# Turning the attention maps of seven units by 32 by 32 squares and two DRAM buffers, in the neighbourhood attention layer

## The reference, cut to what matters

```
q, k, v, g = jnp.split(h @ w_in, 4, axis=-1)           # 16 heads of 64, 4 rows of 64 positions
s_loc = einsum(q, keys in the window) + rpb bias        # 4 rows x 16 columns around the query
s_ctx = einsum(q, kc)                                   # 256 context keys
p = softmax(concat([s_loc, s_ctx]))
o = p_loc @ v + p_ctx @ vc
y = (o * silu(g)) @ w_out
```

## Time and profile before

| | us |
|---|---|
| median of 3 runs | 1815.25 (1814.78 to 1815.6) |
| the profiled execution | 1815.61 |
| its span | 1813.8 |
| DVE busy | 954.2 |
| ACT busy | 901.5 |
| POOL busy | 1366.0 |

### The profile page before, as it was taken

How to read it: one execution, slowest core, us unless ns; L and a number is a source line. 1 busy time by engine, 2 the same in 40 slices (tenths; PEclk the granted TensorE clock), 3 DMA queues, 4 the chain that set the end, 5 groups by cost and what they waited for, 6 DMA issues and landing times.

```text
span 1813.8 us, 24988 instructions
## 1 busy us (share of the span) xinstructions
PE 1793.3 (99%) x9274; PEld 1477.5 (81%) x9274; DVE 954.2 (53%) x1756; ACT 901.5 (50%) x1329; POOL 1366.0 (75%) x568
## 2 busy tenths in 40 slices
PE   6999999999999999999999999999999999999999
PEld 5888888887889888887788888888888878888887
DVE  4673766778755524866653230713095876143152
ACT  3324424674455644456554644464445565555452
POOL 2624544559968898977689798969897867888885
PEclk9999999999999999999999999999999999999999
DMA  9863885749775775565665566567655666656663
GB/s 366 291 210 94 270 310 163 198 141 312 244 277 200 211 221 191 180 198 168 209 186 192 179 195 191 193 187 234 191 193 185 192 190 182 196 160 210 190 195 128
DMA packets 206457, 372.91 MB, mean 206 GB/s; under 512 B 33508, under 2 KB 59092, under 8 KB 205780
## 3 DMA queue, kind: packets, MB, share of 16 engines
q1 hardware_dynamic: 203328, 363.69, 63.5%
q10 hardware_dynamic: 3028, 7.86, 1.2%
HBM read 367.27 MB, written 9.28 MB: 208 GB/s over the span
## 4 chain that ended last, share of the span: by engine, by line
PE 97%; DVE 2%; DMA 0%; issue 0%; ACTq 0%; ACT 0%; POOL 0%; DVEq 0%
PE ps L1300 26%; PE ps L1302 25%; PE ps L1301 25%; PE ps L1426 3%; PE ps L1427 3%; PE ps L1428 3%; PE ps L1992 1%; PE ps L1993 1%; PE ps L1994 1%; PE ps L1348 1%; PE ps L1697 1%; PE ps L1918 1%; PE ps L1668 1%; PE ps L1678 1%; PE ps L1962 1%; PE ps L1558 1%
## 5 line engine op out<-in xcount | busy, mean ns | idle before, releaser
L659 POOL TENSOR_TENSOR w_lo<-raw,w_hi 128x1024 fp32r<-128x1024 f32 x556 | 1347.1, 2461 | 397.4 <-ACT w_hi L697 376.2
L1300 PE MATMUL ps<-w_hi,act_rows_r 128*128 128x512 f32 x2064 | 814.8, 395 | 3.2 <-POOL w_lo L659 3.1
L1302 PE MATMUL ps<-w_hi,act_rows_r 128*128 128x512 f32 x2064 | 805.2, 390 | 0.0
L1301 PE MATMUL ps<-w_lo,act_rows_r 128*128 128x512 f32 x2064 | 804.6, 390 | 0.0
L697 ACT ACTIVATE w_hi<-raw 128x1024 fp32r<-128x1024 f32 x556 | 571.1, 1058 | 371.0 <-DMA raw<-in_ffn_w_up 100.8
L1300 PEld LDWEIGHTS ps<-w_hi,act_rows_r 128*128 128x128 f32 x2064 | 388.2, 188 | 90.4 <-issue 9.1
L1302 PEld LDWEIGHTS ps<-w_hi,act_rows_r 128*128 128x128 f32 x2064 | 388.0, 188 | 82.0
L1301 PEld LDWEIGHTS ps<-w_lo,act_rows_r 128*128 128x128 f32 x2064 | 388.4, 188 | 77.7
L2647 DVE STREAM_TRANSPOSE ps<-proj 32x256 f32<-32x256 f32 (+1 forms) x384 | 166.5, 434 | 6.5
L2628 DVE TENSOR_TENSOR proj<-proj,ps 128x1024 f32<-128x1024 f32 (+1 forms) x18 | 20.4, 1132 | 252.2 <-PE ps L1302 247.9
L1426 PE MATMUL ps<-act_rows_r,w_hi 128*128 128x512 f32 (+1 forms) x288 | 101.3, 352 | 0.0
(11 more groups left out here) (245 smaller groups left out, 1554.0 us busy)
## 6 DMA issues: line engine op xcount, KB each, us to landing
raw<-in_w_in SPq DMA_DIRECT2D x120, 512.0 KB, 3.9
raw<-in_ffn_w_gate SPq DMA_DIRECT2D x88, 512.0 KB, 4.4
raw<-in_ffn_w_up SPq DMA_DIRECT2D x88, 512.0 KB, 4.4
raw<-in_ffn_w_down SPq DMA_DIRECT2D x88, 512.0 KB, 4.2
proj<-in_ada_w SPq DMA_DIRECT2D x39, 512.0 KB, 7.9
pt<-in_ada_w SPq DMA_DIRECT2D x38, 512.0 KB, 6.4
raw<-in_pool_w_in SPq DMA_DIRECT2D x32, 512.0 KB, 7.3
raw<-in_na_w_in SPq DMA_DIRECT2D x32, 512.0 KB, 4.9
```

Source lines behind the costliest of these rows:

```text
L659: pool.tensor_tensor(w_lo[:, s, :], raw[:, s, :], w_hi[:, s, :].bitcast(F32), ALU.subtract).then_inc(lo_done, 1)
L1300: pe.matmul(o, h, hi, start=start, stop=False)
L1301: pe.matmul(o, h, lo, start=False, stop=False)
L1302: return pe.matmul(o, c, hi, start=False, stop=stop)
```

## The change: what it does

For the seven units 0, 2, 4, ..., 12 (`NA_SQUARED`) the maps are no longer turned on PE. DVE transposes the 32 by 32 squares of the whole 128 by 1024 row buffer in one instruction (`na_sq`), into `bias` columns 2048 on; SP writes the 512 KB to one of two DRAM buffers (`keep_squares`) and reads them back in four transfers of 128 KB into `proj` (`place_squares`), where there is one place for them; PE waits for these and reads them with a stride. The two copies out of PSUM (DVE and ACT) go for these units. Their values come two iterations later: at i = u + 5 in place of u + 3, and `na_due(i)` says which units are due. So no values stand at i = 3, and at i = 17 there are those of units 12 and 14: unit 12's come first, ahead of the turn of unit 15, and stay in bank 2.

The row buffer of a squared unit is read by DVE's transpose, so ACT's `na_c` three units later waits for `na_sq`.

`load_bias` now loads, for each pair, four windows of 64 by 219 elements (rows of 876 bytes) into a place in `proj`, and `masked` reads these and writes `bias`, in two instructions of 128 by 512. The load of a pair waits for the mask of two pairs before; the mask, no longer the load, waits until the units of two pairs before have used their bias. The loads of pairs 0 and 1 move from group 7 to group 12 of this layer. `keep_rel` moves out of the attention: one call in the first feed-forward net of each later layer, behind the weights of pair 0.

```diff
+NA_SQUARED = (0, 2, 4, 6, 8, 10, 12)
+    na_squares = nc.dram_tensor("na_squares", (2, P, 1024), F32, kind="Internal").ap()
+        def na_due(i):
+            return [u for u in range(NA_UNITS - 1) if u + (5 if u in NA_SQUARED else 3) == i]
             def load_bias(hp):
-                for h, t, rq in ((h, t, rq) for h in range(2) for t in range(NT) for rq in range(2)):
-                    ...
+                if hp >= 2:
+                    sp.wait_ge(bias_masked, hp - 1)
+                for h in range(2):
+                    for rq in range(2):
+                        src = bass.AP(na_rows.tensor, (2 * hp + h) * RPB_HEAD + (5 - rq) * RPB_C + 15, [[NA_ROW - 1, GRID_W], [1, RPB_SPAN]])
+                        sp.dma_start(bias_windows(hp, [[1, RPB_SPAN]], h * 256, slice(64 * rq, 64 * rq + 64)), src).then_inc(bias_in[hp % 2], 16)
+            def keep_squares(u):
+                sp.wait_ge(dve_done, dve_s.count(("na_sq", u)))
+                if u >= 4:
+                    sp.wait_ge(na_placed, 64 * (u // 2 - 1))
+                sp.dma_start(na_squares[u // 2 % 2], bias[:, 2048:3072]).then_inc(na_kept, 16)
+            def place_squares(u):
+                sp.wait_ge(na_kept, 16 * (u // 2 + 1))
+                if u:
+                    sp.wait_ge(pe_done, pe_s.count(("na_out", u - 2)))
+                for kq in range(4):
+                    sp.dma_start(na_placed_rows([[256, 4], [1, 256]], 0, slice(32 * kq, 32 * kq + 32)),
+                                 bass.AP(na_squares.tensor, u // 2 % 2 * P * 1024 + 256 * kq, [[1024, 32], [32 * 1024, 4], [1, 256]])).then_inc(na_placed, 16)
             for j in range(8):
+                squared = 2 * j - 2 in NA_SQUARED
+                if squared:
+                    keep_squares(2 * j - 2)
                 if j < 6:
-                    sp.wait_ge(dve_done, dve_s.count(("na_l", 2 * j + 1)))
                     load_bias(j + 2)
                 send(I["na_w_out"][0][j * P:(j + 1) * P, :], [[1, D]])
-                if j in (1, 3):
-                    keep_rel(j // 2)
+                if squared:
+                    place_squares(2 * j - 2)
             def masked(hp):
-                pool.tensor_tensor(both, both, free(na_mask[:, 0:1], [[0, 4], [1, SEQ]]), ALU.add).then_inc(bias_masked, 1)
+                if hp >= 2:
+                    pool.wait_ge(dve_done, dve_s.count(("na_l", 2 * hp - 3)))
+                for t in range(NT):
+                    last = pool.tensor_tensor(free(bias[:, 0:1], [[512, 2], [GRID_W, 4], [1, GRID_W]], (hp % 2) * 1024 + t * SEQ),
+                                              bias_windows(hp, [[256, 2], [RPB_C, 4], [1, GRID_W]], 2 * RPB_C * (1 - t)), ...)
         ACT, per unit:
-                        if i >= 3:
+                        if i - 3 in NA_SQUARED:
+                            act.wait_ge(dve_done, dve_s.count(("na_sq", i - 3)))
+                        elif i >= 3:
                             act.wait_ge(pe_done, pe_s.count(("na_t", i - 3, 1)))
         PE, values of a unit:
+                if u in NA_SQUARED:
+                    pe.wait_ge(na_placed, 64 * (u // 2 + 1))
+                        maps = na_placed_rows([[256, 4], [1, 32]], 32 * (4 * c + k)) if u in NA_SQUARED else pt[:, o:o + P]
         PE, loop over i:
-                    if i >= 2:
+                    due = na_due(i)
+                    for u in due[:-1]:
+                        na_values(u)
+                    if i >= 2 and i - 2 not in NA_SQUARED:
                         na_turned(i - 2)
-                    if i >= 3:
-                        na_values(i - 3)
+                    for u in due[-1:]:
+                        na_values(u)
         DVE, in turned(u):
+                    if u in NA_SQUARED:
+                        dve.wait_ge(act_done, act_s.count(("na_e", u, 1)))
+                        if u:
+                            dve.wait_ge(na_kept, 16 * (u // 2))
+                        dve.transpose(free(bias[:, 0:1], [[32, 8], [256, 4], [1, 32]], 2048),
+                                      na_rows_of(u, [[P, 8], [32, 4], [1, 32]])).then_inc(dve_done, dve_s.one(("na_sq", u)))
```

More of the change, by code:

```diff
@@ L23 @@
 RPB_HEAD = 15 * RPB_C
+RPB_SPAN = 5 * RPB_C + GRID_W
 LAYERS = 2
@@ L625, in ffn_weights @@
                                 send(v[:, c:c + 2, pair * 512:(pair + 1) * 512], [[512, 2], [1, 512]])
+                        if tables and pair == 0:
+                            keep_rel(l)
                         if tables and pair < 3:
@@ L662, in masked @@
             def masked(hp):
-                pool.wait_ge(bias_in[hp % 2], 128 * (hp // 2 + 1))
-                both = free(bias[:, 0:1], [[SEQ, 4], [1, SEQ]], (hp % 2) * 1024)
-                pool.tensor_tensor(both, both, free(na_mask[:, 0:1], [[0, 4], [1, SEQ]]), ALU.add).then_inc(bias_masked, 1)
+                pool.wait_ge(bias_in[hp % 2], 64 * (hp // 2 + 1))
+                if hp >= 2:
+                    pool.wait_ge(dve_done, dve_s.count(("na_l", 2 * hp - 3)))
+                for t in range(NT):
+                    last = pool.tensor_tensor(free(bias[:, 0:1], [[512, 2], [GRID_W, 4], [1, GRID_W]], (hp % 2) * 1024 + t * SEQ),
+                                              bias_windows(hp, [[256, 2], [RPB_C, 4], [1, GRID_W]], 2 * RPB_C * (1 - t)),
+                                              free(na_mask[:, 0:1], [[0, 2], [GRID_W, 4], [1, GRID_W]]), ALU.add)
+                last.then_inc(bias_masked, 1)
             pool.wait_ge(dve_done, dve_s.count(("first_gains", 0, 1)))
@@ L962, in na_layer @@
                         u = i - 2
[L963 to L967, removed]
+                        if u not in NA_SQUARED:
+                            act.wait_ge(pe_done, pe_s.count(("na_t", u, 1)))
+                            if u >= 2 and u - 2 not in NA_SQUARED:
+                                act.wait_ge(pe_done, pe_s.count(("na_out", u - 2)))
+                            act.activation(pt[:, (u % 2) * 1024 + 512:(u % 2) * 1024 + 1024], ps[:, 7, :],
+                                           ACT.Copy).then_inc(act_done, act_s.one(("na_pt", u, 1)))
                         if i == NA_UNITS:
@@ L1696, in na_values @@
                         o = (u % 2) * 1024 + c * 512 + k * P
-                        last = pe.matmul(ps[c * HD:(c + 1) * HD, bank, 0:P], v, pt[:, o:o + P], start=k == 0, stop=k == 3)
+                        maps = na_placed_rows([[256, 4], [1, 32]], 32 * (4 * c + k)) if u in NA_SQUARED else pt[:, o:o + P]
+                        last = pe.matmul(ps[c * HD:(c + 1) * HD, bank, 0:P], v, maps, start=k == 0, stop=k == 3)
                 last.then_inc(pe_done, pe_s.one(("na_out", u)))
@@ L2438, in turned @@
                 def turned(u):
[L2439 to L2442, removed]
+                    if u in NA_SQUARED:
[4 more added lines that the diff above has]
+                                      na_rows_of(u, [[P, 8], [32, 4], [1, 32]])).then_inc(dve_done, dve_s.one(("na_sq", u)))
+                    else:
+                        dve.wait_ge(pe_done, pe_s.count(("na_t", u, 0)))
+                        if u >= 2 and u - 2 not in NA_SQUARED:
+                            dve.wait_ge(pe_done, pe_s.count(("na_out", u - 2)))
+                        dve.tensor_copy(pt[:, (u % 2) * 1024:(u % 2) * 1024 + 512], ps[:, 6, :]).then_inc(dve_done, dve_s.one(("na_pt", u, 0)))
                     dve.wait_ge(act_done, act_s.count(("na_e", u, 1)))
@@ L2490, in na_layer @@
                         dve.wait_ge(pe_done, pe_s.count(("na_s", i)))
-                        if i >= 3:
+                        if i >= 3 and i - 3 not in NA_SQUARED:
                             dve.wait_ge(pe_done, pe_s.count(("na_t", i - 3, 1)))
@@ L2504, in na_layer @@
                         gated(0)
+                    due = na_due(i)
+                    for u in due[:-1]:
+                        values(u)
                     if i >= 2:
@@ L2508, in na_layer @@
                         gate_made(7)
-                    if i >= 3:
-                        values(i - 3)
+                    for u in due[-1:]:
+                        values(u)
                     if i == NA_UNITS // 2 - 1:
```

30 lines of the change are left out of this document (17 added, 13 removed).

## The result

The changed kernel takes 1821.34 us (median; 1819.47 to 1826.86) against 1815.25 of the kernel before (1814.56 to 1815.95): ratio 1.0039, interval 1.003 to 1.0049. It is slower, where I had forecast 4 us less. The ratios take in all runs of a kernel, and where a few are long they lie nearer to the means than to the medians (here the means are 7.0 us apart, the medians 6.1). One run of 4383.75 us in the last set and one of the kernel before beside it (2922.31) were in a far slower state and stand in no ratio. The changed kernel's profiled execution was its slowest (1826.86, span 1824.7; before 1815.61, span 1813.8); the same kernel profiled a second time took 1818.71.

What follows compares the result with a forecast made beforehand. PE, busy 99% of the span, was taken to bound the kernel. Turns removed 6.30 less 0.8 (start), 1.1 (unit 12) and 0.4 (scaling) gave 4.0 us less: 1811.3 us, range 1809.2 to 1815.2.

Steps and rivals of the forecast that it cites:

- Turns removed: PE in the attention loop: seven units' turns leave its list, 6.30 us gained.
- Strided reads: PE's values of the squared units: reading the maps with a stride costs nothing; bound, a loss of 7.6 us.
- Start stalls: Iterations 2 and 3: PE comes earlier and waits before scores 3 and 4, 0.8 us lost (0.3 to 1.6).
- Steady iterations and trips of units 2 to 10: Attention loop: bias adds stay hidden and DRAM round trips of units 0 to 10 fit, costing nothing.
- Rival (b): PE before each of seven squared values: round trips don't fit, slower, 1834 at landings of 8.1 us; chance 0.08.
- cover of 2.9 us: Units 0 to 10: time left over after the DRAM trip before PE needs the values, 2.9 us.
- Unit 12: Loop's end: its trip needs 4.05 us, its values stand 2.93 later; PE waits 1.1 us (0.7 to 2.2).
- Scaling: DVE's gate scaling before the squares of units 8 and 10, beside POOL's masks: 0.4 us lost together.
- rival (a): Iteration 12, or 10 and 12: gate scaling meets POOL; 1812.6 for one meeting, 1814.3 for both; chance 0.25.
- Moved loads and table copies: Bias loads at group 12, table copies in the feed-forward net: nothing on PE, bounds 0 and 3 us.
- Nothing idle behind 376 us: After the attention: PE stands idle nowhere it did not before; otherwise the prediction is wrong.
- rival (d): Later stages: earlier PE meets something not earlier, such as weights behind table copies; 3 us back, 1814.3; chance 0.10.

Runs made afterwards that it cites:

- the best version: Changed kernel with gate scaling in iterations 11 and 13, unit 12's values behind the third output group, and POOL waiting for DVE's first feed-forward product: 1811.74 us, ratio 0.9985.
- the hold: Changed kernel with POOL waiting, before group 1's low part in the first feed-forward net, until DVE's first product is done: 1820.44 us; also added to other versions.

## Why the prediction was wrong

**Turns removed: right.** 6.3 us forecast. The landmark gives the closing of the sum: from the loop's first scores to it the best version is 2.9 shorter, and 6.3 less the start stalls (0.5 shown, about 1.0 with what is no wait row) less unit 0's 2.0 is 3.3. Strided reads are free: a squared unit's values at 368.18 are followed by the next piece at 369.20, 1.02 later. The squares took 1.23 us against 1.25 to 1.3, no more under a running POOL. Duration ns, min/median/max:
```profile
L2500 DVE STREAM_TRANSPOSE bias<-full x5: 1230/1235/1236, 313.3 to 364.9; 128x1024 f32<-128x1024 f32 x5
```

**Start stalls: right,** about 1.0 against 0.8: 0.21 and 0.48 as waits of PE at the turn of rows and at scores.

**Steady iterations and trips of units 2 to 10: right where the scaling is moved.** There no wait stands before their values; with the scaling in its place unit 8 waited 0.6 to 1.1 us in six profiles of seven. Rival (b) is not seen, though landings were slower than I took. I had claimed unit 0 with them, and that failed: it waits 1.3 (0.9 to 2.0 in the profiles where SP's order is that of the change). SP's timeline shows four bias loads and a weight send between its keep and its placing:
```profile
314.53 0.35 SPq L601 DMA_DIRECT2D na_squares<-bias  x1
314.92 2.53 SPq L491 DMA_DIRECT2D proj<-na_rows  x4
317.50 1.28 SPq L470 DMA_DIRECT2D raw<-in_na_w_out  x1
318.83 1.86 SPq L609 DMA_DIRECT2D proj<-na_squares  x4
```
My cover of 2.9 us was for a placing at the keep plus 3.0; here it is at plus 4.3, and the landings are longer than 2.3. The cover was also smaller for this unit: PE stood ready for it 8.6 us after the keep, at 323.15, and reached unit 2's values 11.3 us after their keep (321.03 to 332.34, with the 1.3 of unit 0's wait in it). Iteration 3 has no values (1.02 us), which I had used for the start and forgot here.

**Unit 12: the step that failed most,** 1.1 forecast (0.7 to 2.2) and 5.5 measured. The mechanism was right and both its sizes were off. First, the trip. The values of unit 10 end at 369.27 and SP places at once:
```profile
366.17 0.34 SPq L601 DMA_DIRECT2D na_squares<-bias  x1
...
369.36 1.91 SPq L609 DMA_DIRECT2D proj<-na_squares  x4
```
The values start at 375.66: 6.4 us from the free place in place of 4.05, and the 2.35 more make 1.1 into 3.47, the wait of the timeline. The time from issue to landing of all transfers of the two DRAM buffers, min/median/max, shows it:
```profile
DMA to landing us min/median/max: 2.7/3.8/4.8
```
(The placings alone have 2.8/3.9/4.8, and the 4.8 is the last of unit 12, issued at 370.8.) In the mixer the placings have 2.1/2.3/3.5, for transfers three quarters as long; the DMA share was 0.94 at 370 us, but in the mixer too it is 0.89 at 865 us, so that alone does not explain it. I had the bias loads' 8.1 as a warning in rival (b) and did not let it widen this term. Second, the clock: 1.6 us of PE at its lower level behind the wait. No term of the sum had it, because in the profile before PE never stood idle in the attention, and no row there shows what an idle stretch costs. 3.47 + 1.6 = 5.1, near 5.5. Whether the clock falls there is luck of the execution: it did in five of six profiles with this wait, and with the scaling moved it stayed up once (1815.41) and fell once, with the hold (1817.17).

**Scaling: 0.4 forecast, 3.1 measured;** rival (a) is what happened, and its first place was not i = 12 but i = 10, where I had found 0.2 us between. DVE and POOL in iteration 10, and DVE's pair of iteration 12 (356.16):
```profile
345.13 3.94 DVE L2533 SCALAR_TENSOR_TENSOR proj<-proj,rstat 128x256 f32<-128x256 f32 x2
348.99 1.23 DVE L2500 STREAM_TRANSPOSE bias<-proj 128x1024 f32<-128x1024 f32 x1
...
356.16 1.74 DVE L2533 SCALAR_TENSOR_TENSOR proj<-proj,rstat 128x256 f32<-128x256 f32 x2
...
343.93 2.34 POOL L709 TENSOR_TENSOR bias<-proj,na_mask 128x512 f32<-128x512 f32 x2 [3.38 <-DMA proj<-na_rows]
346.23 2.56 POOL L700 TENSOR_TENSOR w_lo<-raw,w_hi 128x1024 fp32r<-128x1024 f32 x1
```
The masks had waited 3.38 us for their windows, so they and the low part ran under the scaling; its second instruction came through at the low part's end, the squares behind it 2.9 us late, and PE waited 2.14. The wait was not for bias add 13, as I had it, but for the copy that stands behind the squares in DVE's list (the output of unit 7, L2491). With the lower clock behind it that passes the 1.7 that I allowed one meeting; in the second profile, where the clock stayed up, it is 1.40 here and 0.80 at unit 8. At i = 12 the pair took 1.74 and cost nothing seen.

**Moved loads and table copies: right at nothing** on the path (1815.14 with no squares), but only as an edit by itself: with the squares, moving the table copies out of the attention is worth 19 us.

**Nothing idle behind 376 us: wrong.** I had kept 3 us in rival (d) for a later loss, behind weights or table copies. The loss is there, but of another kind: in the feed-forward net the shifted POOL and DVE meet at a product on PE's path. It is there in some executions and not in others. It costs 0.9 to 2.8 in the medians of the change, 5.3 in the median and 2.9 in the mean with unit 12 last and the scaling moved, nothing with unit 12 turned, and 5.0 in the profile shown (5.9 with the wait of 0.88 at 590.16, which the hold does not take away: 0.56 is left in the best version).

The sum as it should have been: 3.45 gained (1815.19 - 1811.74, start and unit 0 in it), less 5.5, 3.1 and some 1 to 3 for the lock: 6 to 8 us slower, as measured in the two sets of runs (6.1 and 8.3).

Left open: what decides whether the clock falls behind a wait of 2 to 3.5 us; what decides whether DVE gets in between two of POOL's back-to-back instructions, which at 379.62 before it did and at 592.69 it did not; and what lengthens the landings from 2.3 to 3.8 us, since moving the gate rows did not. A different SP order for unit 0 that does not delay unit 2 was not tried.

## What to carry to other kernels

Price a wait before an otherwise full PE with the clock behind it: here idle stretches of 2.1 to 3.5 us cost some 1.6 us more in most profiles, and nothing in others. A round trip through DRAM costs little where two iterations of cover stand behind it (six trips cost some 1 to 2 us here, most of it at unit 0) and much in the one unit at the loop's end where they don't (5.5); judge that unit by itself, with landing times of the stretch it lies in, and leave it out or give its consumer a later slot. And when a change shifts DVE against POOL by a few us, look far behind the change at every DVE operation with two SBUF operands on PE's path; one wait that makes POOL pause there may be worth more than the change.

## What was not expected of the hardware

A 0.69 us DVE operation stood 7.33 us while the rest of one GpSimd instruction and two more of 2.36 us went ahead of it, in some executions of one kernel and not in others; eleven runs of one version fell into groups 5 us apart, and making POOL pause there took the slower group away but for one run. Transposes of 32x32 blocks from SBUF to SBUF stayed at 1.23 us whatever POOL did. With table copies from DRAM to DRAM right ahead of small transfers on one queue, PE waited up to 10 us for these. After 3.04 us idle the granted clock stayed at 1.00 in one execution, after 2.14 in another it fell to the 1.2 GHz level.
